# A hybrid decoder layer on one core: weight loads issued by ScalarE, a reordered first norm, sample rows scaled by VectorE, the first weight load in two pieces

## The reference, cut to what matters

```
def rmsnorm(x, g):
    xf = x.astype(jnp.float32)
    y = xf * lax.rsqrt(jnp.mean(xf * xf, axis=-1, keepdims=True) + EPS)
    return (y * g.astype(jnp.float32)).astype(x.dtype)
...
    h = rmsnorm(x, norm_mix_pre)
    proj = h @ w_in
    q, k, v, z, xbc, dt_raw, g_attn, g_ssm = jnp.split(proj, _split_points(), axis=-1)
...
    attn = moba_attention(q, k_all, v_all, q_pos0)
    ssm, conv_new, ssm_new = mamba2_branch(z, xbc, dt_raw, conv_prev, ssm_prev, ...)
    merged = jax.nn.sigmoid(g_attn) * (attn @ w_attn_out) + jax.nn.sigmoid(g_ssm) * (ssm @ w_ssm_out)
    x = x + rmsnorm(merged @ w_out, norm_mix_post)
    f = swiglu(rmsnorm(x, norm_ffn_pre), w_gate, w_up, w_down)
    x = x + rmsnorm(f, norm_ffn_post)
```

## Time and profile before

| what | value |
|---|---|
| time, median of 3 runs | 1876.82 us (1874.03 to 1877.71) |
| time of the profiled execution itself | 1878.19 us |
| its span in the profile | 1876.1 us |
| PE busy | 1820.2 us (97%) |
| DVE busy | 1207.4 us (64%) |
| ACT busy | 859.6 us (46%) |
| POOL busy | 204.6 us (11%) |
| transfers | 417.01 MB, 222 GB/s |

### The profile page before, as it was taken

One profiled execution on the slowest core, in us unless ns is written; L12 is line 12 of the kernel. 1 busy time (PEld: TensorE's weight loads), 2 busy tenths in 40 slices (PEclk: granted clock), 3 DMA queues, 4 the chain that ended last, 5 costly groups with the idle time before them and its releaser, 6 DMA issues.

```text
span 1876.1 us, 35069 instructions
## 1 busy us (share of the span) xinstructions
PE 1820.2 (97%) x14759; PEld 1741.3 (93%) x14759; DVE 1207.4 (64%) x1675; ACT 859.6 (46%) x1445; POOL 204.6 (11%) x124
## 2 busy tenths in 40 slices
PE   6999999999999999999999999999999999999997
PEld 5999998998988988888999899999999999999997
DVE  4368888899897656754664556676665666444444
ACT  5454455544444343543444455454454544434442
POOL 2144444354000000000000000000000000000000
PEclk9999999999999999999999999999999999999998
DMA  6578887888569798968556367777777777656552
GB/s 201 171 253 284 299 288 214 266 272 267 174 192 289 237 294 251 336 210 270 180 173 211 113 214 214 226 221 234 226 229 215 222 234 216 205 173 188 159 180 90
DMA packets 385996, 417.01 MB, mean 222 GB/s; under 512 B 10544, under 2 KB 363728, under 8 KB 384752
## 3 DMA queue, kind: packets, MB, share of 16 engines
q1 hardware_dynamic: 385280, 413.98, 69.9%
q0 software_dynamic: 208, 0.67, 0.2%
q10 hardware_dynamic: 352, 0.12, 0.0%
HBM read 396.37 MB, written 18.63 MB: 221 GB/s over the span
## 4 chain that ended last, share of the span: by engine, by line
PE 80%; DVE 11%; DMA 4%; ACT 3%; issue 2%; SPq 0%; ACTq 0%; POOL 0%; DVEq 0%; POOLq 0%
PE gemm L1617 25%; PE gemm L1618 24%; PE gemm L1619 24%; DVE w_lo L1109 5%; PE side L1584 2%; PE side L1872 2%; DMA brows<-bc_row 2%; DMA out_ssm_sample<-st 1%; DVE sc_flat L1290 1%; ACT w_hi L732 1%; DVE conv_out L1103 1%; PE side L1585 1%; DMA cst_w<-in_conv_w 1%; ACT att_s L732 1%; PE side L1893 0%
## 5 line engine op out<-in xcount | busy, mean ns | idle before, releaser
L1109 DVE TENSOR_TENSOR w_lo<-raw,w_hi 128x1024 fp32r<-128x1024 f32 (+1 forms) x562 | 734.1, 1322 | 470.0 <-ACT w_hi L732 469.1
L1617 PE MATMUL gemm<-x_hi,w_hi 128*128 128x264 f32 x3344 | 970.8, 290 | 29.1 <-DVE w_lo L1109 27.7
L1619 PE MATMUL gemm<-x_hi,w_lo 128*128 128x264 f32 x3344 | 951.7, 285 | 0.0
L1618 PE MATMUL gemm<-x_lo,w_hi 128*128 128x264 f32 x3344 | 951.2, 284 | 0.0
L732 ACT ACTIVATE w_hi<-raw 128x1024 fp32r<-128x1024 f32 (+1 forms) x562 | 574.2, 1042 | 336.1 <-PE gemm L1619 334.1
L1617 PEld LDWEIGHTS gemm<-x_hi,w_hi 128*128 128x128 f32 x3344 | 633.8, 190 | 59.5 <-DVE w_lo L1109 32.4
L1618 PEld LDWEIGHTS gemm<-x_lo,w_hi 128*128 128x128 f32 x3344 | 634.9, 190 | 1.2 <-issue 0.5
L1619 PEld LDWEIGHTS gemm<-x_hi,w_lo 128*128 128x128 f32 x3344 | 631.4, 189 | 0.0
L1618 PE MATMUL gemm<-g_lo,w_hi 128*128 128x264 f32 x704 | 200.5, 285 | 0.0
L1617 PE MATMUL gemm<-g_hi,w_hi 128*128 128x264 f32 x704 | 200.2, 284 | 0.0
L1619 PE MATMUL gemm<-g_hi,w_lo 128*128 128x264 f32 x704 | 199.6, 284 | 0.0
(11 more groups left out here) (305 smaller groups left out, 1378.4 us busy)
## 6 DMA issues: line engine op xcount, KB each, us to landing
raw<-in_w_in SPq DMA_DIRECT2D x104, 1024.0 KB, 6.6
raw<-in_w_gate SPq DMA_DIRECT2D x44, 1024.0 KB, 5.5
raw<-in_w_up SPq DMA_DIRECT2D x44, 1024.0 KB, 5.3
raw<-in_w_down SPq DMA_DIRECT2D x40, 1024.0 KB, 5.4
kv<-in_cache_k SPq DMA_DIRECT2D x64, 512.0 KB, 5.8
kv<-in_cache_v SPq DMA_DIRECT2D x64, 512.0 KB, 4.7
st<-in_state_ssm SPq DMA_DIRECT2D x64, 256.0 KB, 5.5
raw<-in_w_ssm_out SPq DMA_DIRECT2D x16, 1024.0 KB, 6.5
```

Of the source, the lines that this page charges most:

```text
L1109: v.tensor_tensor(w_lo[:, s, 0:blk.kts, cols], raw[:, s, 0:blk.kts, cols], w_hi[:, b % RING, 0:blk.kts].bitcast(fp32), ALU.subtract).then_ ...
L1617: mm(out, w_hi[:, b % RING, k], pr.hi[:, x], start=(x == 0), stop=False)
L1618: mm(out, w_hi[:, b % RING, k], pr.lo[:, x], start=False, stop=False)
L1619: ins = mm(out, w_lo[:, s, k, cols], pr.hi[:, x], start=False, stop=(x == pr.kt - 1))
```

## The change

Four things are changed together.

1. **Who issues weight loads.** SP still issues loads 0 to 4. Each later load is issued by ScalarE, right behind the `w_hi` of the block whose wait has shown the slot free (`first_free`). SP runs `side_work(b)` as soon as `mm_done` is b, without weight loads between.
2. **The first norm.** Each chunk of prompt rows is squared half by ScalarE and half by VectorE. VectorE's half, divided by D and with EPS added, goes in as the bias of the root. PE runs 16 matmuls of `ident` by `ident` at the start and 6 more ahead of the first `x_turn` (`warm`), whose output nobody reads.
3. **Sample rows.** VectorE scales them instead of ScalarE, PE turns all 16 tiles at once into one bank, and gain, `x_hi` and `x_lo` are made for all of them in one instruction each. An `x_turn` is two instructions instead of three.
4. **Transfers at the start.** Load 0 comes in two pieces of 128 columns, block 0 waits for the first alone. Load 1 still waits for all constants. The `cst_w` transpose moves into block 0 (k = 4), its copy `conv_k` behind it. GpSimd's two transfers of `state_conv` wait for load 0.

```diff
+        def weights(n):
+
+            p, kg = loads[n]
+            pr = pairs[p]
+            kts = min(KG, pr.kt - KG * kg)
+            src = pr.w[kg * KG * P:(kg * KG + kts) * P, pr.col:pr.col + P * pr.halves]
+            return raw[:, n % LOADS, 0:kts, 0:P * pr.halves], src.rearrange("(k p) n -> p k n", p=P)
+
+        first_free = {}
+        for n in range(LOADS, len(loads)):
+            first_free.setdefault(last_of_load[n - LOADS] + RING, []).append(n)
...
+        sq_s = junk3[0:NB, :]
+        xs_t = junk[:, 1, 0:KT * NB].rearrange("p (k b) -> p k b", b=NB)
...
-                if n >= LOADS:
-                    sp.wait_ge(mm_done, last_of_load[n - LOADS] + 1)
-                if n == 1:
-                    sp.wait_ge(rows_in, 16 * 7)
-                sp.dma_start(raw[:, s, 0:kts, 0:P * pr.halves], src.rearrange("(k p) n -> p k n", p=P))\
-                    .then_inc(loaded[s], 16)
...
-            seen = 0
-            for n in range(len(loads)):
-                weights(n)
-                if n >= LOADS:
-                    now = last_of_load[n - LOADS] + 1
-                    for b in range(seen, now + 1):
-                        side_work(b)
-                    seen = now + 1
-            for b in range(seen, END):
+            for n in range(LOADS):
+                if n == 0:
+                    dst, src = weights(0)
+                    sp.dma_start(dst[:, :, 0:P], src[:, :, 0:P]).then_inc(raw_first, 16)
+                    sp.dma_start(dst[:, :, P:2 * P], src[:, :, P:2 * P]).then_inc(loaded[0], 16)
+                    continue
+                if n == 1:
+                    sp.wait_ge(rows_in, 16 * 6)
+                    sp.wait_ge(wrow_in, 16)
+                sp.dma_start(*weights(n)).then_inc(loaded[n], 16)
+            for b in range(END):
+                wait(sp, mm_done, b)
                 side_work(b)
...
-            gp.dma_start(ctok[:, :], a["state_conv"][0].rearrange("b w c -> (b w) c")).then_inc(state_in, 16)
-
-            gp.dma_start(o["conv_sample"][0, :, 0:2, :], a["state_conv"][0, :, 1:3, :]).then_inc(cs_out, 16)
...
+            gp.wait_ge(loaded[0], 16)
+            gp.dma_start(ctok[:, :], a["state_conv"][0].rearrange("b w c -> (b w) c")).then_inc(state_in, 16)
+            gp.dma_start(o["conv_sample"][0, :, 0:2, :], a["state_conv"][0, :, 1:3, :]).then_inc(cs_out, 16)
...
+                if b == 0:
+                    act.wait_ge(raw_first, 16)
+                elif blk.n == 0 or b == 1:
                     act.wait_ge(loaded[s], 16 * (blk.load // LOADS + 1))
                 wait(act, mm_done, b - RING + 1)
                 func(w_hi[:, b % RING, 0:blk.kts], raw[:, s, 0:blk.kts, blk.n * P:(blk.n + 1) * P]).then_inc(hi_done, 1)
+                for n in first_free.get(b, ()):
+                    act.dma_start(*weights(n)).then_inc(loaded[n % LOADS], 16)
...
-            act.wait_ge(x_rs, 1)
-            func(xtok[0:NB, 2, :], xtok[0:NB, 2, :], scale=nrs[0:NB, 0, 2:3]).then_inc(x_half0, 1)
             act.wait_ge(x_in[0], 16)
-            drained(func(junk[:, 0, :], xtok[:, 0, :], ACT.Square, accum_out=nsum[:, 0, 0:1]))
-            func(nsd[:, 0, 0:1], nsum[:, 0, 0:1], ACT.Sqrt, bias=eps[:, 0:1], scale=1.0 / D).then_inc(x_sd, 1)
+            drained(func(junk[:, 0, 0:1024], xtok[:, 0, 0:1024], ACT.Square, accum_out=nsum[:, 0, 0:1]))
+            act.wait_ge(x_sum2, 2)
+            func(nsd[:, 0, 0:1], nsum[:, 0, 0:1], ACT.Sqrt, bias=nsum[:, 3, 0:1], scale=1.0 / D).then_inc(x_sd, 1)
             act.wait_ge(x_rs, 2)
-            for n in range(2):
-                half = xtok[:, 0, n * 1024:(n + 1) * 1024]
-                func(half, half, scale=nrs[:, 0, 0:1]).then_inc(x_half0, 1)
-            act.wait_ge(x_sum2, 2)
-            func(nsd[:, 0, 1:2], nsum[:, 0, 1:2], ACT.Sqrt, bias=eps[:, 0:1], scale=1.0 / D).then_inc(x_sd, 1)
+            func(xtok[:, 0, 0:1024], xtok[:, 0, 0:1024], scale=nrs[:, 0, 0:1]).then_inc(x_half0, 1)
+            act.wait_ge(x_in[1], 16)
+            drained(func(junk[:, 0, 1024:2048], xtok[:, 1, 0:1024], ACT.Square, accum_out=nsum[:, 0, 1:2]))
+            act.wait_ge(x_sum2, 3)
+            func(nsd[:, 0, 1:2], nsum[:, 0, 1:2], ACT.Sqrt, bias=nsum[:, 3, 1:2], scale=1.0 / D).then_inc(x_sd, 1)
+            func(xtok[:, 0, 1024:2048], xtok[:, 0, 1024:2048], scale=nrs[:, 0, 0:1]).then_inc(x_half0, 1)
             act.wait_ge(cst_t, 1)
             func(gains[:, :, :], gemm_ps[0][:, 0:5 * XT].rearrange("p (n k) -> p n k", k=XT)).then_inc(rows_cp, 1)
             func(conv_bias[:, :], gemm_ps[0][:, 5 * XT:7 * XT], scale=0.5).then_inc(rows_cp, 1)
-            act.wait_ge(cst_t, 2)
-            func(conv_k[:, :, :], gemm_ps[1][:, 0:P].rearrange("p (n k) -> p n k", k=CT), scale=0.5).then_inc(rows_cp, 1)
-            act.wait_ge(rows_cp, 3)
+            act.wait_ge(xs_dve, 2)
+            func(x_hi[:, :, TP:T], xs_t).then_inc(xs_act, 1)
...
+                if b == 0:
+                    act.wait_ge(cst_t, 2)
+                    func(conv_k[:, :, :], gemm_ps[1][:, 0:P].rearrange("p (n k) -> p n k", k=CT), scale=0.5)\
+                        .then_inc(rows_cp, 1)
+                    act.wait_ge(rows_cp, 3)
...
+            stt(sq_s, xtok[0:NB, 2, :], 1.0, xtok[0:NB, 2, :], ALU.mult, ALU.mult,
...
-            dve.wait_ge(x_sd, 2)
-            v.reciprocal(nrs[:, 0, 0:1], nsd[:, 0, 0:1]).then_inc(x_rs, 1)
-            dve.wait_ge(x_in[1], 16)
-            dve.wait_ge(x_sum2, 1)
-            stt(junk[:, 1, :], xtok[:, 1, :], 1.0, xtok[:, 1, :], ALU.mult, ALU.mult,
-                accum_out=nsum[:, 0, 1:2]).then_inc(x_sum2, 1)
-            dve.wait_ge(x_sd, 3)
-            then(dve, v.reciprocal(nrs[:, 0, 1:2], nsd[:, 0, 1:2]), x_rs, 3)
+            dve.wait_ge(consts_made, 3)
+            for c in range(2):
+                dve.wait_ge(x_in[c], 16)
+                half = xtok[:, c, 1024:2048]
+                drained(stt(junk2[:, c, :], half, 1.0, half, ALU.mult, ALU.mult, accum_out=nsum[:, 1, c:c + 1]))
+                v.tensor_scalar(nsum[:, 3, c:c + 1], nsum[:, 1, c:c + 1], 1.0 / D, eps[:, 0:1], ALU.mult, ALU.add)\
+                    .then_inc(x_sum2, 1)
+                dve.wait_ge(x_sd, 2 + c)
+                then(dve, v.reciprocal(nrs[:, 0, c:c + 1], nsd[:, 0, c:c + 1]), x_rs, 2 + c)
+                if c == 0:
+                    v.tensor_scalar(xtok[0:NB, 2, :], xtok[0:NB, 2, :], nrs[0:NB, 0, 2:3], None, ALU.mult)\
+                        .then_inc(xs_dve, 1)
             for n in range(2):
                 half = xtok[:, 1, n * 1024:(n + 1) * 1024]
                 v.tensor_scalar(half, half, nrs[:, 0, 1:2], None, ALU.mult).then_inc(x_half1, 1)
-            dve.wait_ge(rows_cp, 3)
+            dve.wait_ge(rows_cp, 2)
+            dve.wait_ge(xs_pe, 1)
+            then(dve, v.tensor_tensor(xs_t, gemm_ps[1][:, P:2 * P].rearrange("p (k b) -> p k b", b=NB),
+                                      gains[:, 0, :].unsqueeze(2).to_broadcast([P, KT, NB]), ALU.mult), xs_dve, 2)
+            dve.wait_ge(xs_act, 1)
+            v.tensor_tensor(x_lo[:, :, TP:T], xs_t, x_hi[:, :, TP:T].bitcast(fp32), ALU.subtract).then_inc(xs_dve, 1)
...
+                            if x == 4:
+                                pe.wait_ge(wrow_in, 16)
+                                turn(gemm_ps[1][:, 0:P], cst_w[:, :]).then_inc(cst_t, 1)
...
-                pe.wait_ge(x_half0, k // 8 + 2)
+                pe.wait_ge(x_half0, k // 8 + 1)
                 turn(bank[:, 0:P], xtok[:, 0, cols])
                 pe.wait_ge(x_half1, k // 8 + 1)
-                turn(bank[:, P:2 * P], xtok[:, 1, cols])
-                turn(bank[:, TP:T], xtok[0:NB, 2, cols]).then_inc(x_tr, 1)
+                turn(bank[:, P:2 * P], xtok[:, 1, cols]).then_inc(x_tr, 1)
...
+            def warm(count):
+
+                for _ in range(count):
+                    mm(gemm_ps[3][:, 0:P], ident[:, :], ident[:, :], start=True, stop=True)
+
             pe.wait_ge(consts_made, 2)
-            pe.wait_ge(rows_in, 16 * 7)
+            warm(16)
+            pe.wait_ge(xs_dve, 1)
+            for k in range(KT):
+                ins = turn(gemm_ps[1][:, P + k * NB:P + (k + 1) * NB], xtok[0:NB, 2, k * P:(k + 1) * P])
+            ins.then_inc(xs_pe, 1)
+            pe.wait_ge(rows_in, 16 * 6)
             turn(gemm_ps[0][:, 0:7 * XT], cst_v[:, :]).then_inc(cst_t, 1)
-            turn(gemm_ps[1][:, 0:P], cst_w[:, :]).then_inc(cst_t, 1)
+            warm(6)
             for k in range(6):
                 x_turn(k)
-            pe.wait_ge(rows_cp, 3)
+            pe.wait_ge(rows_cp, 2)
+            pe.wait_ge(xs_dve, 3)
```

28 lines of the change are left out of this document (16 added, 12 removed).

## The result

| | before | after |
|---|---|---|
| median | 1877.26 us (1874.03 to 1882.67, 4 runs) | 1860.88 us (1857.63 to 1861.55, 4 runs) |
| profiled execution, its span | 1878.19, 1876.1 us | 1860.62, 1858.6 us |

The ratio is 0.9907, with a 95% interval of 0.9892 to 0.9921: faster by 0.9%, twice the forecast, and 0.1 us outside the range.

The account below looks back on a forecast made before the run. PE, busy 97% of the span, was taken to bound the kernel. Gains of 2.5 + 2.9 + 0.3 + 2.6 = 8.3 us against the median of 1876.82 gave 1868.5 us, range 1861 to 1875.

Parts of the forecast that it names:

- Part 1: Start of the kernel: PE's first product comes at 18.6 instead of 21.14 us, a gain of 2.5 us.
- Part 2: Block 0: pitch per tile falls from 1.59 to 1.15 us, gaining 2.9 us, with 0.3 us more in block 2.
- If the clock rises as before: Blocks 0 and 1: clock rises only after 3 us of products alone, so the start gains 5.7 us in all.
- rival B: Clock rises in the middle of block 0: 3.0 us more gain, 1865.5 us, chance 0.28.
- The bound of the range: Fast end of the range: a clock up at the first product gives some 1.5 us more, so 1861 us.
- My argument against B: Start, before block 0: 6 us of transposes (15.0 to 21.1) had not raised the clock.
- My other argument: Start: the first 16 `ident` matmuls are followed by 5 us in which PE has nothing.
- Part 3: First key page: `q_row` and its chain move 3.2 us earlier, removing PE's wait of 2.6 us, a gain of 2.6 us.
- Part 4: Weight loads: ScalarE issuing 277 of the 282 gives nothing, at 0.385 us per issue.
- Rival E: Issues on ScalarE delay the work behind them: slower, 1881 to 1893.5 us, chance 0.09.
- Apart from part 3 PE's waits are for VectorE's own bursts. I take nothing.: Rest of the kernel: SP's side transfers coming one block earlier were counted as no gain.
- The shifting: Across the kernel: PE's other waits may move, counted as nothing with a margin of +-3 us.

Follow-up runs that it names:

- e11: The change with load 0 in one piece again, GpSimd's state transfers still waiting for it: 1857.85 us, 0.9897 of before.
- e3: The change without its 22 `warm` matmuls of `ident`: 1861.47 us, 0.9908 of before.
- e9: e3 with a third, unread transpose of the sample rows put back into each `x_turn`: 1869.27 us, 0.9954 of before.
- e1: Before, with ScalarE issuing the loads from number 5 on and SP's side work run block by block, old start: 1871.79 us, 0.9969 of before.
- e4: The change with SP issuing every load, each at its own `mm_done`, side work block by block: 1856.63 us, 0.9890 of before.
- e8: The change, ScalarE still issuing loads, but SP's side work in steps of a whole load as before: 1866.81 us, 0.9950 of before.
- f6: e4 with GpSimd's multiply of each key page cut to 64 of 1024 columns: 1843.62 us, 0.9813 of before.
- f2: The change with GpSimd's multiply of each key page cut to 64 of 1024 columns: 1842.16 us, 0.9802 of before.
- e7: The change with each of ScalarE's loads as two transfers of half the rows, 554 issues instead of 277: 1853.69 us, 0.9875 of before.
- e10: The change with GpSimd's two state transfers back at the start, load 0 still in two pieces: 1860.75 us, 0.9904 of before.
- f3: The change run again unaltered, on another chip: 1860.52 us, 0.9902 of before.
- e11b: The change with load 0 in one piece and GpSimd's two state transfers back at the start: 1863.19 us, 0.9915 of before.
- e2: The change with the loads back in SP's stream and side work behind them, new start kept: 1869.19 us, 0.9955 of before.
- f4: e4 with every load from the fifth on as two transfers: 1858.86 us, 0.9897 of before.
- f1: Before, with GpSimd's multiply of each key page cut to 64 of 1024 columns: 1856.84 us, 0.9883 of before.

## Why the prediction was wrong, step by step

The direction was right, and the moves of parts 1 to 3 all took place. All three came out too small, above all since the clock did not rise "as before"; one term was taken as nothing, and a loss was not seen. That the time still lies only 0.1 us outside the range is luck: 14.0 us of gain were missed, and 4.8 us of loss.

- **Part 1, first product at 18.6, 2.5 us.** It started at 17.71: 3.4 us. x1 landed 0.8 us earlier, where I had left it: VectorE starts on it at 10.52. It comes earlier in every kernel with the state transfers moved, as shown above. The 16 sample transposes took 1.87 us, and I had taken 3.2; the six `warm` took 2.6 and I had 1.3, since each is two records of 0.21. These two cancel by luck. Load 0 was not waited for, as said, though through the state transfers (e11) more than the pieces.
- **Part 2, 2.9 + 0.3 us: the step that failed most.** "If the clock rises as before" did not hold, and rival B did, with 28% against 38%. But B was too small as well: it let the clock rise in the middle of block 0, and it was up at the first product. From there to block 1, 6.65 us were gained, and 1.2 more in blocks 1 to 3. The start is 11.3 us in place of 5.7. (The bound of the range had that case, with 1.5 us more: 5.7 + 3.0 + 1.5 = 10.2 for the start.) Without the rise the pitch is near what I computed: 1.09 in e3, at the low clock, against 1.15. The pair e3 and e9 shows the cause: of the 11.3 us some 8.5 hang on one small transpose per tile. My argument against B, that 6 us of transposes had not raised the clock before, was an argument for it: if transposes don't raise it, taking some away must be priced at the other clock. My other argument was that PE has nothing for 5 us behind the first 16 matmuls. That pause was 2.3 us: the 16 took 6.2, since each is two records.
- **Part 3, 2.6 us** "since there is no more to win there". The chain moved by the 3.2 us computed, and 4.5 were gained by block 40. I had read PE's waits up to 140 us; two more, 1.6 us in sum, stand at 140 to 160 us in before and belong to the next pages. And that the `w_lo` are late was not only the order in VectorE's stream: 1.0 us was the stretch beside GpSimd's multiply. e1 and e4 show the gain, e8 its absence with late side work.
- **Part 4, nothing for the issuer** held: f6 against f2, and e7 with 554 issues. Rival E is refuted.
- **"Apart from part 3 PE's waits are for VectorE's own bursts. I take nothing."** This failed. In the feed-forward `w_lo` was late because `w_hi` was, and that because ScalarE stood at `brows`: 6.5 us were gained there. I had followed PE's waits one step back and named the engine, but had not gone on to what that engine waited for. ScalarE's longest wait behind the one for PE was this one.
- **The shifting, put at +-3 us,** was -4.7 in blocks 80 to 90, -2.5 in two stretches at half the clock and +2.5 elsewhere, and differed from kernel to kernel: from block 40 to 90 the gain changed by -5.1 (e10) to +3.5 us (e4). The bound came from no row. The stretch was there to be read in before: `w_lo` of up to 3.4 us beside its usual 1.21.

Predicted and measured, in us: start 5.7 and 11.3; key pages 2.6 and 4.5; feed-forward 0 and 6.5; shifts 0 and -4.8. The sums are 8.3 and 17.5.

**What stays open.** Why the half-clock stretches near 800 and 1050 us come both in after, f3, e1, e3, e4, e11b, f2 and f6, only one of them in e2, e8, e9, e10, e11 and f4, and none in before, f1 and e7. Around 796 us PE's waits are the same in before and after (1.7 or 1.8, and 1.1 us). Nor is it settled whether e7 is better than e4; their intervals overlap (0.9857 to 0.9894, 0.9872 to 0.9908). The fastest medians with the whole computation are these two. Both are below the change's, but e4's interval overlaps that of the change (0.9892 to 0.9921), and e7's touches it. What gives e7 its lead over the change is read from its one trace, and no run tests it.

## What to carry to other kernels

A stream that carries both the loads and the small side transfers delays the small ones by its waits. Give each its own wait in the order of need; who issues matters less. Follow each wait of the bounding engine back to the first cause, through every in-order engine, and put the largest waits of the engines behind it on the list before taking a term as nothing. Where TensorE starts at its low clock, price every mix of transposes and products at both clocks, and where GpSimd and VectorE both read two tensors, expect a change of phase to move the time by several microseconds either way. And before a difference of a few microseconds between two profiles is explained, look whether the medians show it.

## What the hardware showed that I had not expected

- With one more transpose of 8 rows per tile (pitch 1.59 us) TensorE stayed at the spacing of 0.22 us for 15.8 us from the first product (e9); without it (pitch 1.09) the spacing fell to 0.12 after 3.0 us (e3).
- The column of the granted clock read 1.00 in that same low stretch of e9, and 0.50 only where the clock had been up before (12 to 16 us in after): the spacing of products is the surer sign.
- An `xdts` of 128x32 took 2.17 us instead of 0.19 beside GpSimd's multiply.
- Two state transfers of 384 and 256 KB, issued at the start, made the first `w_hi`, which waits for a load of 1 MB, start 2.7 us later (17.31 in e11b, 14.60 in e11).
- Both half-clock stretches near 800 and 1050 us came again at the same places in another execution of the same program (f3).
